# Two PSUM banks of their own for the inverse of the delta rule, and three buffers for the rest

## The reference, cut to what matters

```python
a = jnp.where(strict, jnp.einsum('bhnik,bhnjk->bhnij', k_beta, k) * decay, 0.0)
rhs = jnp.concatenate([v_beta, k_beta * jnp.exp(g)[..., None]], axis=-1)
sol = lax.linalg.triangular_solve(a + eye, rhs, left_side=True, lower=True, unit_diagonal=True)
...
def step(s, xs):
    u_c, w_c, qk_c, qd_c, kd_c, gl_c = xs
    v_new = u_c - w_c @ s
    o = qd_c @ s + qk_c @ v_new
    s = s * gl_c[..., None, None] + jnp.swapaxes(kd_c, -1, -2) @ v_new
    return s, o
```

## Time and profile before

| | us |
|---|---|
| median of three runs | 1672.38 (1671.41 to 1674.83) |
| the profiled execution, all of it | 1674.93 |
| its span, first to last instruction | 1673.0 |
| mean granted clock of TensorE | 0.904 of full speed |

### The profile page before, as it was taken

One profiled execution on the slowest core, in us unless ns is written; L12 is line 12 of the kernel. 1 busy time (PEld: TensorE's weight loads), 2 busy tenths in 40 slices (PEclk: granted clock), 3 DMA queues, 4 the chain that ended last, 5 costly groups with the idle time before them and its releaser, 6 DMA issues.

```text
span 1673.0 us, 26759 instructions
## 1 busy us (share of the span) xinstructions
PE 1430.7 (86%) x11370; PEld 1121.6 (67%) x11370; DVE 717.2 (43%) x1224; ACT 408.6 (24%) x574; POOL 98.8 (6%) x160
## 2 busy tenths in 40 slices
PE   5999999997877599659999489989999648999855
PEld 3677777676666377448888367777777437788744
DVE  3377798445552452431111469599110320111116
ACT  3455551123223001311111222732100321111102
POOL 0111122000000000020000200000000020000020
PEclk9999999997877699679999689999999868999986
DMA  9565319300000642289998630003021138999732
GB/s 360 204 252 221 131 51 383 129 27 2 3 2 16 224 145 96 116 336 340 356 354 291 229 155 1 0 27 127 26 76 58 51 136 313 353 354 352 307 119 106
DMA packets 67508, 285.63 MB, mean 171 GB/s; under 512 B 7377, under 2 KB 24017, under 8 KB 43729
## 3 DMA queue, kind: packets, MB, share of 16 engines
q1 hardware_dynamic: 61872, 264.27, 42.6%
q0 software_dynamic: 5536, 19.93, 3.3%
HBM read 232.43 MB, written 51.74 MB: 170 GB/s over the span
## 4 chain that ended last, share of the span: by engine, by line
PE 69%; DVE 16%; DMA 5%; ACT 4%; issue 3%; POOL 1%; SPq 1%; POOLq 0%; DVEq 0%; ACTq 0%
PE acc L698 24%; PE acc L1042 15%; PE acc L1050 7%; PE acc L730 3%; PE acc L1172 2%; PE acc L741 2%; PE acc L718 2%; PE acc L709 2%; PE acc L828 1%; PE acc L1138 1%; DVE big L1877 1%; DVE yT L1904 1%; PE acc L775 1%; ACT hT L1313 1%; DMA yT<-xs 1%
## 5 line engine op out<-in xcount | busy, mean ns | idle before, releaser
L698 PE MATMUL acc<-hT,ring 128*128 128x288 f32 x1792 | 444.0, 409 | 10.0 <-ACT hT L1313 7.8
L698 PEld LDWEIGHTS acc<-hT,ring 128*128 128x128 f32 x1792 | 340.7, 191 | 114.7 <-issue 11.7
L1042 PEld LDWEIGHTS acc<-zT,ring 128*128 128x128 f32 x2176 | 253.5, 195 | 20.4 <-issue 14.3
L1042 PE MATMUL acc<-zT,ring 128*128 128x128 f32 x2176 | 254.4, 279 | 4.6 <-ACT zT L1343 2.3
L1050 PE MATMUL acc<-ring,zT 128*128 128x512 f32 x272 | 124.9, 602 | 8.6 <-DVE zT L2251 2.9
L2251 DVE TENSOR_TENSOR zT<-zT,acc 128x256 f32<-128x256 f32 x32 | 13.5, 421 | 235.0 <-ACT zT L1348 235.0
L2256 DVE COPY yT<-acc 128x1024 f32<-128x1024 f32 x32 | 39.2, 1224 | 124.8 <-PE acc L1050 124.8
L1050 PEld LDWEIGHTS acc<-ring,zT 128*128 128x128 f32 x272 | 48.9, 189 | 64.4 <-issue 62.2
L1348 ACT ACTIVATE zT<-acc 128x256 f32<-128x256 f32 x32 | 12.3, 385 | 316.8 <-PE acc L1042 316.8
L1033 PE MATMUL acc<-cst,yT 128*128 128x128 f32 x272 | 37.6, 284 | 39.0 <-DMA yT<-xs 39.0
L698 PE MATMUL acc<-yT,ring 128*128 128x288 f32 x256 | 63.9, 412 | 0.1
(11 more groups left out here) (441 smaller groups left out, 1852.8 us busy)
## 6 DMA issues: line engine op xcount, KB each, us to landing
ring<-in_w SPq DMA_DIRECT2D x102, 1024.0 KB, 8.0
ring<-in_w_mod_mix SPq DMA_DIRECT2D x24, 1024.0 KB, 9.3
ring<-in_w_mod_ffn SPq DMA_DIRECT2D x24, 1024.0 KB, 6.9
yT<-xs SPq DMA_DIRECT2D x34, 512.0 KB, 8.6
ring<-in_w_in SPq DMA_DIRECT2D x16, 1024.0 KB, 9.1
ys<-yT SPq DMA_DIRECT2D x32, 512.0 KB, 8.0
xs<-S SPq DMA_DIRECT2D x3, 4096.0 KB, 26.2
ring<-in_glu SPq DMA_DIRECT2D x8, 1024.0 KB, 7.8
```

The costliest lines, as they stand in the source:

```text
L698: mm = pe.matmul(ps[:, b, 0:HT], w[:, k, :], rhs[:, k, HT * b:HT * b + HT], start=(k == 0), stop=(k == KD - 1))
L1042: mm = pe.matmul(acc[:, H_ACC, x, P * f:P * (f + 1)], wv[:, f, k, :], xt[:, k, :], start=(k == 0), stop=(k == KD - 1), skip_group_check=True)
```

## The change

One set, number 0, is taken out of the rotation while the inverse runs (`hold("inverse")` beside projection 25, `release` behind `state_v(3)`). All X products and `X_6` go to its first bank, all Q products and `R` to its second; they no longer call `begin`, and wait for no set. The second result of level 5, which lay in the second bank of its set, now lies in the upper half of the same bank as the first. Everything else turns on the three sets that are left until the release. `begin` takes the set that was given back first, and waits for the reader of its last group. ACT and DVE read X and Q from the two banks; otherwise nothing moves.

```diff
+INV_ACC = 0
...
         def buf(name):
 
-            return acc[:, use(name) % NACC, :, :]
+            return acc[:, book.get(("buf", name), 0), :, :]
...
+        x_bank, q_bank = (acc[:, INV_ACC, b, :] for b in range(2))
...
+            def await_reader(i):
+
+                last = state["last"].get(i)
+                if last:
+                    pe.wait_ge(reader(last), at("read:" + last))
+
+            def hold(name):
+
+                i = state["free"].pop(0)
+                await_reader(i)
+                book["buf", name] = i
+                return acc[:, i, :, :]
...
+            def release(name, last=None):
+
+                i = book["buf", name]
+                state["last"][i] = last or name
+                state["free"].append(i)
 
             def begin(name):
 
-                n = state["n"]
-                book["use", name] = n
-                book["name", n] = name
-                if n >= NACC:
-                    last = book["name", n - NACC]
-                    pe.wait_ge(reader(last), at("read:" + last))
-                state["n"] += 1
-                return acc[:, n % NACC, :, :]
+                ps = hold(name)
+                release(name)
+                count(name)
+                return ps
...
-            def diagonal(name, lhsT, rhs):
-
-                ps = begin(name)
+            def diagonal(name, ps, lhsT, rhs):
+
+                count(name)
...
                 if l < NLEV:
-                    diagonal(f"X{t}_{l}", AB5[:, l], Mc)
+                    diagonal(f"X{t}_{l}", x_bank, AB5[:, l], Mc)
                     return
...
                 if l < NLEV:
-                    diagonal(f"Q{t}_{l}", Xc, MTc)
+                    diagonal(f"Q{t}_{l}", q_bank, Xc, MTc)
                     return
...
                 if m == 25:
+                    hold("inverse")
+                    assert book["buf", "inverse"] == INV_ACC, book["buf", "inverse"]
                     prepare(4, 0)
...
             state_v(3)
+            release("inverse", "R3")
             state_o(3)
```

More of the change, by code:

```diff
@@ L675, in _, with count @@
         def _(pe):
-            state = {"n": 0}
-            def begin(name):
-                n = state["n"]
-                book["use", name] = n
-                book["name", n] = name
-                if n >= NACC:
-                    last = book["name", n - NACC]
-                    pe.wait_ge(reader(last), at("read:" + last))
-                state["n"] += 1
-                return acc[:, n % NACC, :, :]
+            state = {"n": 0, "free": list(range(NACC)), "last": {}}
+            def await_reader(i):
[7 more added lines that the diff above has]
+                return acc[:, i, :, :]
+            def count(name):
+                book["use", name] = state["n"]
+                state["n"] += 1
+            def release(name, last=None):
+                i = book["buf", name]
+                state["last"][i] = last or name
+                state["free"].append(i)
+            def begin(name):
+                ps = hold(name)
+                release(name)
+                count(name)
+                return ps
             def weights(n):
@@ L821, in sample_update @@
                                 mm.then_inc(acc_full, 1)
-            def diagonal(name, lhsT, rhs):
-                ps = begin(name)
+            def diagonal(name, ps, lhsT, rhs):
+                count(name)
                 for h in range(H):
                     for q in QUADS:
-                        mm = pe.matmul(ps[q, 0, 32 * h:32 * h + 32], lhsT[q, h, :], rhs[q, h, :], start=True, stop=True,
+                        mm = pe.matmul(ps[q, 32 * h:32 * h + 32], lhsT[q, h, :], rhs[q, h, :], start=True, stop=True,
                                        skip_group_check=True)
@@ L835, in inverse_x @@
                 if l < NLEV:
-                    diagonal(f"X{t}_{l}", AB5[:, l], Mc)
+                    diagonal(f"X{t}_{l}", x_bank, AB5[:, l], Mc)
                     return
-                ps = begin(f"X{t}_{l}")
+                count(f"X{t}_{l}")
                 for h in range(H):
                     for src, dst in ((0, 32), (64, 96)):
-                        mm = pe.matmul(ps[dst:dst + 32, 0, 32 * h:32 * h + 32], AT[t][src:src + 32, h, dst:dst + 32],
+                        mm = pe.matmul(x_bank[dst:dst + 32, 32 * h:32 * h + 32], AT[t][src:src + 32, h, dst:dst + 32],
                                        Mc[src:src + 32, h, :], start=True, stop=True, skip_group_check=True)
@@ L848, in inverse_q @@
                 if l < NLEV:
-                    diagonal(f"Q{t}_{l}", Xc, MTc)
+                    diagonal(f"Q{t}_{l}", q_bank, Xc, MTc)
                     return
-                ps = begin(f"Q{t}_{l}")
+                count(f"Q{t}_{l}")
                 for h in range(H):
                     cols = slice(32 * h, 32 * h + 32)
-                    pe.matmul(ps[0:32, 0, cols], Xc[32:64, h, :], MTc[32:64, h, :], start=True, stop=True,
+                    pe.matmul(q_bank[0:32, cols], Xc[32:64, h, :], MTc[32:64, h, :], start=True, stop=True,
                               skip_group_check=True)
-                    pe.matmul(ps[64:96, 0, cols], Xc[96:128, h, :], MTc[96:128, h, :], start=True, stop=True,
+                    pe.matmul(q_bank[64:96, cols], Xc[96:128, h, :], MTc[96:128, h, :], start=True, stop=True,
                               skip_group_check=True)
-                    mm = pe.matmul(ps[32:64, 1, cols], MTc[32:64, h, :], Xc[32:64, h, :], start=True, stop=True,
-                                   skip_group_check=True)
+                    mm = pe.matmul(q_bank[32:64, 256 + 32 * h:288 + 32 * h], MTc[32:64, h, :], Xc[32:64, h, :],
+                                   start=True, stop=True, skip_group_check=True)
                 mm.then_inc(acc_full, 1)
@@ L865, in inverse_last_x @@
                 pe.wait_ge(inv_assembled, at(f"asm{t}"))
-                ps = begin(f"X{t}_6")
+                count(f"X{t}_6")
                 for h in range(H):
-                    mm = pe.matmul(ps[64:128, 0, 64 * h:64 * h + 64], AT[t][0:64, h, 64:128], half64[0:64, h, :],
+                    mm = pe.matmul(x_bank[64:128, 64 * h:64 * h + 64], AT[t][0:64, h, 64:128], half64[0:64, h, :],
                                    start=True, stop=True, skip_group_check=True)
@@ L874, in inverse_last @@
                 pe.wait_ge(act_drained, at(f"read:X{t}_6"))
-                ps = begin(f"R{t}")
+                count(f"R{t}")
                 for h in range(H):
-                    mm = pe.matmul(ps[0:64, 0, 64 * h:64 * h + 64], half64[64:128, h, :],
+                    mm = pe.matmul(q_bank[0:64, 64 * h:64 * h + 64], half64[64:128, h, :],
                                    MTf[64:128, h, 64:128], start=True, stop=True, skip_group_check=True)
@@ L1054, in moe @@
             def moe(layer):
-                for n in range(state["n"] - NACC, state["n"]):
-                    last = book["name", n]
-                    pe.wait_ge(reader(last), at("read:" + last))
+                for i in range(NACC):
+                    await_reader(i)
                 first = unit_no["moe", layer, 0]
@@ L1458, in x_out @@
                 for rows in ((slice(0, P),) if l < NLEV else (slice(32, 64), slice(96, 128))):
-                    act.activation(Xc[rows], bank(f"X{t}_{l}", 0, P)[rows].rearrange("p a n -> p (a n)")[
-                        :, 0:32 * H].rearrange("p (h n) -> p h n", n=32), ACT.Copy).then_inc(
+                    act.activation(Xc[rows], x_bank[rows, 0:32 * H].rearrange("p (h n) -> p h n", n=32),
+                                   ACT.Copy).then_inc(
                         act_drained, up(act_drained, f"read:X{t}_{l}"))
@@ L1479, in last_block @@
                 act.wait_ge(acc_full, filled(f"X{t}_6"))
[L1480 removed]
+                act.activation(half64[64:128], x_bank[64:128].rearrange("p (h n) -> p h n", n=64), ACT.Copy).then_inc(
                     act_drained, up(act_drained, f"read:X{t}_6"))
                 act.wait_ge(acc_full, filled(f"R{t}"))
[L1483 removed]
+                act.activation(MTf[0:64, :, 64:128], q_bank[0:64].rearrange("p (h n) -> p h n", n=64), ACT.Copy,
                                scale=-1.0).then_inc(act_drained, up(act_drained, f"read:R{t}"))
@@ L2019, in update_blocks @@
                 dve.wait_ge(inv_zeroed, 2)
-                ps = [buf(f"Q{t}_5")[:, b, 0:32 * H].rearrange("p (h n) -> p h n", n=32) for b in range(2)]
+                ps = [q_bank[:, 256 * b:256 * b + 256].rearrange("p (h n) -> p h n", n=32) for b in range(2)]
                 for dst, src in ((half64[32:64, :, 0:32], ps[1][32:64]), (MTf[64:96, :, 96:128], ps[0][64:96]),
```

2 lines of the change are left out of this document (1 added, 1 removed).

## The result

The change makes the kernel faster: 1657.39 us (median of 4 runs, 1655.33 to 1659.32) against 1672.62 for the kernel before, a ratio of 0.9906 with a 95% interval of 0.9894 to 0.9918. A second set of 5 runs of the changed kernel gave 1658.01 (ratio 0.9911, 0.9895 to 0.9926). The forecast was 1656.6. The profiled execution has a span of 1657.3 us, 15.7 less than before. No instruction changed its place on any engine, so the traces can be laid side by side.

A forecast was written before the change was run, and what follows sets the result against it. In the delta rule PE waited for PSUM sets whose readers were late. Gains 2.7 + 10.7 + 1.3 + 0.3 + 0.8 = 15.8 us (bounds 8 to 20), from the median 1672.38, give 1656.6 us; range 1649 to 1667.

The forecast's parts named there:

- `kk`, 10.7 us: Between updates with Q_3 and Q_4: kk starts directly behind Q_3, DVE becomes the bound, its 10.7 us idle goes.
- `br`, 2.7 us: Ahead of Q_3, t = 0 to 2: br waits for DVE's row mask, not o's reader; 2.7 us earlier.
- `ks`, 1.3, and `vt`, 0.3: Behind kk and qk: ks starts earlier, 1.3 us; vt's wait mostly moves to X_6, leaving 0.3 us.
- `Q3_4`, 0.8 us: In t = 3, Q3_4 waits for ACT's copy of X3_4 instead of su2's reader; 0.8 us earlier.
- Nothing lost beside the projections: Beside the last projections, three sets cost nothing; tightest is Z0, covered by 0.56 us of PE's queue.
- The gain passes the reload: Behind o3, the sample state reload (15.23 us wait) is chained to the delta rule's end and moves with it.
- the two clock rivals: PE stays low behind Q_3, 1664 us (chance 0.18); clock also rises in slow pieces, about 1649 us (0.10).
- the one that kept PE low behind `Q_3`: Low clock reaches into kk and qk, 7.3 of 10.7 us lost: gain 8.5, 1664 us; chance 0.18.
- The one that raised the clock from `X_6` to `vn`: X_6, R, X_1 and vn, at 0.50, speed up, returning 6 to 10 us: about 1649 us; chance 0.10.
- The slower rival: PE idle gathers ahead of X_5 and X_6, clock falls for more of the tile: 30 us lost, 1684; chance 0.04.
- The rule of the Trainium skill that spoke against the change: Double-buffering PSUM gave a fed matmul kernel no further gain (125.5 against 126.6 us); here, time near 1672.

The follow-up runs named there:

- the kernel that moves its work: The change, with three pieces of DVE work moved ahead of the update with Q_3: 1651.98 us, ratio 0.987.
- the fillers: Matmuls nobody reads in PE's stalls: added to the change around X_6, 1649.89 us; added in all tiles to the kernel with moved DVE and ACT work, 1637.98 us.
- the two-set kernel: The change, but groups other than X and Q turn on two sets instead of three: 1669.6 us, ratio 0.9986 to the kernel before.
- the kernel with late `ks` and `vt`: The change, but ks1, ks2 wait for qk's reader and vt1 to vt3 for kt's reader as before: 1661.49 us, ratio 0.9926.
- two of the experiments: The change with two sets for the other groups, 1669.6 us; and the change with kk1 to kk3 waiting for their old readers, 1666.49 us.

## Why the prediction was right

By its own steps, with the span of the delta rule as the measure:

- *`kk`, 10.7 us*: the three stretches are 10.7 us shorter, and DVE has no idle time left in them but the steps between instructions. DVE as the next bound is shown by the kernel that moves its work: the same stretches then fall to 5.3 us, PE's list (5.4 was said). Taking `kk`'s earlier start away alone makes them 9.1 us longer again.
- *`br`, 2.7 us*: `br` is released by the row mask (L1937) as said. Taking it away alone lets DVE idle 0.60, 0.96 and 0.96 us more, where 0.67, 1.04 and 1.03 were said.
- *`ks`, 1.3, and `vt`, 0.3*: from the update with `Q_4` to `X_6` it was 6.15, 8.60 and 8.32 us in t = 0, 1, 2, and is 6.15, 7.63 and 7.62 now: 1.7 us, where 1.6 were said. Undone alone in the changed kernel they cost more, since `ks` falls to the low clock behind the stalls and the late `vt` holds `X_6` up; that price was not in the sum.
- *`Q3_4`, 0.8 us*: the updates around it are 3.93 us apart instead of 4.76, as said; t = 3 as a whole is 0.5 us shorter.
- *Nothing lost beside the projections*: `Z0` starts 0.56 us after the end of ACT's reading of `p26` (314.58 + 0.65 = 315.23), the cover that was said, and it held:

```profile
314.58 0.65 ACT L1571 ACTIVATE zT<-acc 128x576 f32<-128x576 f32 x1
...
315.79 1.08 PE L827 MATMUL acc<-ring,yT 128*32 128x128 f32 x32
```

- *The gain passes the reload*: it moved by 16.35 us and is waited for about as long.

The whole is nearer to the forecast than each tile's way to it. The tiles t = 1 and t = 2 gave 5.1 and 5.5 us, where the sum has 5.2 and 5.9, but in t = 1 two shifts of the clock, which the sum does not have, cancel. `vn0` ran lower than before, and from `X_1` to the update with `Q_3` that tile is 0.2 us longer (17.21 for 16.99), `br`'s gain eaten up; `X1_6` and `R1` ran higher, which gave 1.1 us. `vn0`, `X1_6` and `R1` before, and `vn0` after (the other two stand above):

```profile
413.32 2.88 PE L730 MATMUL acc<-ring,yT 128*128 128x128 f32 x16
...
447.12 1.97 PE L868 MATMUL acc<-half,hT 64*64 64x64 f32 x16
...
449.77 1.97 PE L877 MATMUL acc<-yT,half 64*64 64x64 f32 x16 [0.68 <-ACT half L1480]
```

```profile
408.09 3.78 PE L753 MATMUL acc<-ring,yT 128*128 128x128 f32 x16
```

The second execution of the change reads the same there (`vn0` 3.78, `X1_6` 1.14, `R1` 1.84 us). That the two cancel is luck; the steps above do not rest on it.

Of the two clock rivals, the one that kept PE low behind `Q_3` did not come: `kk` to `Q_4` ran at 1.00. The one that raised the clock from `X_6` to `vn` did not come either, but for `X1_6` and `R1`: `vn` takes 3.78 us in t = 0 to 2. Its price, 6 to 10 us, was sound: the fillers bought back 7.5 to 8 us from two tiles, and 10.6 with t = 0 and t = 3. The slower rival's time does not follow from its own terms: 30 us lost against 15.8 gained is about 1687 us, not 1684. And the earlier trace rows shows the clock up to the stall for t = 1 alone; the trace has 1.00 for t = 2 too (456 to 473 us).

The rule of the Trainium skill that spoke against the change ("TensorE: Matmul & The Clock Gate", "HAM oscillation — how this bites in real kernels": a second PSUM buffer gained nothing more) does not carry over: the third set gave 12 to 13 of the 15 us here. The Trainium skill's section "A second HAM failure mode: psum-queue depth-cycling" ("TensorE: Matmul & The Clock Gate"), on short idles between groups that make the clock oscillate, fits `ks1` above (3.55 instead of 2.05 us behind two stalls of 0.7 and 0.6 us).

What stays open: what the two-set kernel kept, 2.3 us (0.3 to 4.5 by its interval). In its trace `Q3_4` has its 0.8 us (updates 3.89 us apart instead of 4.76), and the clock fell elsewhere than before (1.00 instead of 0.81 between the two updates of t = 1, 0.70 instead of 0.84 in t = 0); one trace of each cannot say whether that is the rest.

## What to carry to other kernels

A rotation over n buffers counts every user. Where short-lived products alternate with long-lived ones, the long-lived ones get half the depth; giving the chain, which never overlaps itself, a fixed buffer is cheaper than it looks, because the chain needs no rotation. To price such a change, take not the waits that go (some 20 us here, 9.4 of them at `kk` and 4.0 at `vt`) but the idle time of the engine that comes next in that stretch, and check that its list of work is the longer one. Then look for what the clock does behind the stalls that stay: it moved single stretches here by about 1 us either way.

## What the runs showed of the hardware

A stall of PE can cost more than its length. In the kernel with late `ks` and `vt`, a wait of 0.6 us ahead of `ks1`, close behind another of 0.7, made DVE wait 2.2 us longer, because the group behind it ran at 1.2 GHz (granted clock 0.53; 3.55 us instead of 2.05). It need not: behind the same stall of 2.3 us ahead of `kk2`, the clock was 0.81 over the stretch in the kernel before and 1.00 in two of the experiments.

Matmuls that nobody reads, in stalls that were there anyway, returned 7.5 to 8 us with fillers in mainly two tiles (mean granted clock 0.88 from 380 to 520 us, 0.80 and 0.82 in the two traces of the change) and 10.6 us with fillers in all (0.97 instead of 0.84 from 380 to 500 us). One ahead of `X_6` in t = 0, behind a group that was slow already, left `vn0` at 3.78 us; four in t = 1 and in t = 2 brought `vn` to 2.02.
